# A two-block float32 transformer on one core: VectorE and ScalarE work in another order around the output projections and the recurrent preparation, with fewer unread products

## The chip, the cores and the metric

One core of a Trainium2 chip runs the whole program in one launch. The time is device microseconds (us) of that launch. In the profile PE is TensorE's matmuls, PEld its weight loads, DVE is VectorE, ACT ScalarE, POOL GpSimd, SP SyncE.

## The reference

Two residual blocks run over a sequence of 256 positions of width 1024. The change touches the end of the first block's mixer and the first layer of the second:

```python
merged = jax.nn.sigmoid(gate_a) * (y_a @ w_a_out) + jax.nn.sigmoid(gate_b) * (y_b @ w_b_out)
return merged @ w_out
...
y = h @ w_in                                   # second block, 272 positions
ys = ys + (prev - ys) * mu
r, k, v, wd, ad, gd = jnp.split(ys, RWKV_SPLITS, axis=-1)
decay = jnp.exp(-jnp.exp(wlog))
kk = kk / jnp.maximum(jnp.linalg.norm(kk, axis=-1, keepdims=True), 1e-12)
kf = kf * (1.0 + (a - 1.0) * k_a)
...
S = S * w_t + sa[..., None] * (kk_t * a_t) + v_t[..., None] * k_t
o = jnp.einsum('bhvk,bhk->bhv', S, r_t)
...
bonus = jnp.sum(rf * kf * r_k, axis=-1, keepdims=True) * vf
o = (o + bonus) * g
```

Everything is float32. The reference steps through the positions one by one; the kernel takes them in chunks of 128, 128 and 16 with a triangular inverse per head.

## The kernel before, in words

**Weights.** All weights come as slabs of 8 x 128 rows by 256 columns through a ring of four buffers `raw`. ScalarE rounds a slab to the high part (`split_hi`, L465), VectorE subtracts to get the low part (`split_lo`, L473), and TensorE makes three products per tile: high by high, low activation by high weight, high activation by low weight (`pe_pairs`, L560 to L562), 48 for a slab. There are two buffers of `w_hi` and `w_lo`, so a slab can be split as soon as the one two before it has been multiplied (`slab_done`). A section of a projection is a list of slabs; the slab with number u fills two PSUM banks, which must have been emptied (`act_took`, `dve_took`) two slabs before.

**Order.** The order is written out by hand: each engine has its own program, and semaphores tie them together. `act_pairs` and `dve_pairs` write one section for ScalarE and VectorE: for each slab u they split the next slab and then take the outputs of slab u-1. ScalarE and VectorE run what they are given strictly in this order.

**Output projections** (about 510 to 612 us). Sections `a_out` (four half slabs), `b_out` (four slabs) and `w_out` (four). VectorE multiplies the outputs of `a_out` with their gate (`gated_a`, L2079) and so frees their banks; it makes the low half of `y_b` in two halves (`low_b`, L2098) from `yb_hi`, which ScalarE writes (L2024). TensorE begins `b_out` with tiles in order, three products each, and waits at a tile for its low half `yb_l`. For each slab of `b_out`, `gated_b` multiplies the outputs by their gate into `tmp_b` (L2115), adds (`merged`, L2118), waits for ScalarE's rounded copy `x_hi` (`high`, L2032), and subtracts to `x_lo` (L2120). `w_out` begins tile by tile behind these.

**Recurrent preparation** (to 892.9 us). Sections `ev_s` (seven slabs) and `ev_u` (two). ScalarE copies outputs out (`copy`, L2268), VectorE mixes each position with the one before it (`shifted`, L2324 and L2326); beside them stand a norm of `kk` (a reciprocal square root on ScalarE, L2301, then three VectorE operations, L2367 to L2370), the decays (four exponentials on ScalarE, L2294 to L2298), and at the end six products on VectorE and the bonus product on `v_t` (L2382). After `ev_u` TensorE makes 28 products that nobody reads (`HATS_BUSY`, L527, `keep_busy`).

**Recurrent block** (893.2 to 999 us). VectorE makes `hats`, ScalarE copies two Gram matrices into `rb_at` (L2698), VectorE begins the inverse (`begin`, L1021 to L1028), then five levels follow: products `products_p`, masks on VectorE, a further Gram matrix (`later`), products `products_y`, `grow`. Unread products stand in the waits: `TURN_BUSY` 3 at each level and 12 more at the first, which with 3 make the 15 of one row. Then come three steps (`step_of`), each: right side, `ww` solve, new state, outputs `oo`; with `STEP_BUSY` = 8 unread products behind the right side, 8 behind the solve, 8 before the outputs, and one within each second head of the outputs.

## Time and profile before

| | us |
|---|---|
| median of 3 runs | 1616.67 (1611.66 to 1644.3) |
| the profiled execution, its own time | 1619.03 |
| its span, first to last instruction | 1617.2 |
| mean granted TensorE clock | 0.988 of full |

Busy time of an engine is time with an instruction in it. An idle interval in brackets names what ended it. `PEq` or "issue" means that no data dependency is shown for it. Matmul ends are modelled; their starts, and the starts of the weight loads, are what a pace is read from.

### The profile page before, as it was taken

To read this page: it belongs to the slowest core of one execution; us is meant where nothing else is said; L and a number is where in the kernel's file an instruction comes from. 1 tells how busy PE (TensorE), PEld (TensorE's weight loads), DVE (VectorE), ACT (ScalarE), POOL (GpSimd) and SP (SyncE) were. 2 spreads that over 40 slices of the span, in tenths; PEclk is the share of its full clock that TensorE was granted. 3 is DMA by queue.
4 is the path that set the end of the run, shared out by engine and by line. 5 is a ranking of instruction groups with operands and counts; after the bars stand their busy time and mean duration, and the time that the engine had idled before them with its cause. 6 is when DMAs were issued, how large, how long until landed. Compare 5 with 4: busy or idle time off the path is not lost. (4 is left out here: it accounts for less than half of the span.)

```text
span 1617.2 us, 33845 instructions
## 1 busy us (share of the span) xinstructions
PE 1541.4 (95%) x14269; PEld 1486.2 (92%) x14269; DVE 1042.7 (64%) x1584; ACT 741.4 (46%) x1024; POOL 61.1 (4%) x82
## 2 busy tenths in 40 slices
PE   5999999999999899999999999999999998899997
PEld 5999998999999898999989998999998987799997
DVE  7999546998754768444488855645446666565544
ACT  2555435695214734444356022566333354456532
POOL 0111000000110000110000100000000000000000
PEclk9999999999999999999999999999999999999999
DMA  9899645543213446555443002354452431245551
GB/s 376 302 357 355 233 170 186 183 157 119 74 61 105 169 157 234 183 182 189 177 132 117 10 2 76 109 182 161 177 183 87 145 117 52 79 157 182 184 187 47
DMA packets 39201, 256.88 MB, mean 159 GB/s; under 512 B 4259, under 2 KB 5668, under 8 KB 9892
## 3 DMA queue, kind: packets, MB, share of 16 engines
q1 hardware_dynamic: 37492, 251.07, 43.1%
q10 hardware_dynamic: 1584, 3.97, 0.6%
q8 instruction: 100, 1.64, 0.4%
q14 instruction: 25, 0.20, 0.0%
HBM read 251.87 MB, written 3.15 MB: 158 GB/s over the span
## 5 line engine op out<-in xcount | busy, mean ns | idle before, releaser
L473 DVE TENSOR_TENSOR w_lo<-raw,w_hi 128x2048 fp32r<-128x2048 f32 (+2 forms) x203 | 456.3, 2248 | 407.6 <-ACT w_hi L465 407.1
L560 PE MATMUL bank<-x_hi,w_hi 128*128 128x256 f32 (+1 forms) x1832 | 524.9, 287 | 17.6 <-DVE w_lo L473 7.4
L465 ACT ACTIVATE w_hi<-raw 128x2048 fp32r<-128x2048 f32 (+2 forms) x203 | 381.7, 1880 | 315.0 <-PE bank L562 291.1
L562 PE MATMUL bank<-x_hi,w_lo 128*128 128x256 f32 (+1 forms) x1832 | 516.8, 282 | 0.0
L561 PE MATMUL bank<-x_lo,w_hi 128*128 128x256 f32 (+1 forms) x1832 | 516.3, 282 | 0.0
L560 PEld LDWEIGHTS bank<-x_hi,w_hi 128*128 128x128 f32 x1832 | 345.9, 189 | 26.2 <-issue 16.3
L562 PEld LDWEIGHTS bank<-x_hi,w_lo 128*128 128x128 f32 x1832 | 348.1, 190 | 0.0
L561 PEld LDWEIGHTS bank<-x_lo,w_hi 128*128 128x128 f32 x1832 | 346.3, 189 | 0.9 <-issue 0.7
L560 PE MATMUL bank<-mh_hi,w_hi 128*128 128x272 f32 (+1 forms) x512 | 145.6, 284 | 0.0
L562 PE MATMUL bank<-mh_hi,w_lo 128*128 128x272 f32 (+1 forms) x512 | 145.6, 284 | 0.0
L561 PE MATMUL bank<-mh_lo,w_hi 128*128 128x272 f32 (+1 forms) x512 | 145.5, 284 | 0.0
L560 PE MATMUL bank<-hid_hi,w_hi 128*128 128x256 f32 x352 | 98.8, 281 | 1.6 <-DVE w_lo L473 1.6
L561 PE MATMUL bank<-hid_lo,w_hi 128*128 128x256 f32 x352 | 98.3, 279 | 0.0
L562 PE MATMUL bank<-hid_hi,w_lo 128*128 128x256 f32 x352 | 98.3, 279 | 0.0
L562 PEld LDWEIGHTS bank<-mh_hi,w_lo 128*128 128x128 f32 x512 | 97.3, 190 | 0.0
L560 PEld LDWEIGHTS bank<-mh_hi,w_hi 128*128 128x128 f32 x512 | 96.2, 188 | 0.0
L561 PEld LDWEIGHTS bank<-mh_lo,w_hi 128*128 128x128 f32 x512 | 96.2, 188 | 0.0
L560 PEld LDWEIGHTS bank<-hid_hi,w_hi 128*128 128x128 f32 x352 | 66.6, 189 | 2.4 <-issue 2.4
L1173 ACT ACTIVATE hid_hi<-hid 128x256 f32 (+1 forms) x44 | 18.4, 418 | 105.5 <-DVE hid L1214 105.5
L561 PEld LDWEIGHTS bank<-hid_lo,w_hi 128*128 128x128 f32 x352 | 66.3, 188 | 0.0
L562 PEld LDWEIGHTS bank<-hid_hi,w_lo 128*128 128x128 f32 x352 | 66.3, 188 | 0.0
L3178 PE MATMUL bank<-x_hi,w_hi 128*128 128x272 f32 (+1 forms) x192 | 61.4, 320 | 4.9 <-DVE k_at L3316 3.4
(593 smaller groups left out, 2525.0 us busy)
## 6 DMA issues: line engine op xcount, KB each, us to landing
raw<-in_stream SPq DMA_DIRECT2D x227, 1024.0 KB, 4.8
raw<-in_stream SPq DMA_DIRECT2D x8, 768.0 KB, 4.0
gate_store<-stage ACTq DMA_DIRECT2D x8, 256.0 KB, 2.5
raw<-in_stream SPq DMA_DIRECT2D x4, 512.0 KB, 3.4
h<-in_h ACTq DMA_DIRECT2D x1, 1088.0 KB, 9.1
zt<-gate_store SPq DMA_DIRECT2D x1, 1024.0 KB, 5.5
gate<-gate_store SPq DMA_DIRECT2D x1, 1024.0 KB, 7.7
out<-h SPq DMA_DIRECT2D x8, 128.0 KB, 1.9
```

Source lines behind the costliest of these rows:

```text
L465: nc.scalar.activation(w_hi[:, s_at % 2, 0:kt], raw[:, r_at % RING, 0:kt], ACT.Copy).then_inc(hi_done, 1)
L473: nc.vector.tensor_tensor(w_lo[:, s_at % 2, 0:kt], raw[:, r_at % RING, 0:kt], w_hi[:, s_at % 2, 0:kt].bitcast(F32), ALU.subtract).then_inc ...
L560: nc.tensor.matmul(out, hi, xh[:, k0 + k, 0:L], start=start, stop=False)
L561: nc.tensor.matmul(out, hi, xl[:, k0 + k, 0:L], start=False, stop=False)
L562: mm = nc.tensor.matmul(out, lo, xh[:, k0 + k, 0:L], start=False, stop=stop)
L1173: nc.scalar.activation(hid_hi[:, bass.ds(n, 1)], hid[:, b:b + 1], ACT.Copy).then_inc(hid_h, 1)
L3178: nc.tensor.matmul(out, hi, x_hi[:, k, cols], start=k == 0, stop=False)
```

## The change

In the output projections: `b_out` begins in three phases (all high by high products, then all low by high, then all by the low weights), each with its own wait; `gated_a(2)` goes ahead of both `low_b`, and both go ahead of the low weights of `b_out`; in `b_out` the gates of a slab go ahead of the split of the next one, and the next slab's high part on ScalarE goes ahead of the last `high`. In the preparation: the root of `kk` goes ahead of the exponentials on ScalarE; its three VectorE operations go ahead of the last `shifted` and of the split; the bonus product goes to the recurrent block, behind `hats`. There the first later Gram matrix uses banks 2 and 3, the inverse begins half by half, the last split of `ev_u` moves from the beginning to level 3 and the window part 3 (`v_t`) behind the levels. Unread products: `HATS_BUSY` 28 to 4, the 12 at level 0 gone, behind the right side 8 to 3 (`SOLVE_BUSY`), before and within the outputs 10 to 0 in each of two steps: 24 + 12 + 10 + 20 = 66 fewer. Nothing that is computed changes.

```diff
-TURN_BUSY, FIRST_TURN_BUSY, HATS_BUSY, STEP_BUSY, END_BUSY, OUT_BUSY, MIX_BUSY = 3, 12, 28, 8, 24, 14, 26
+TURN_BUSY, FIRST_TURN_BUSY, HATS_BUSY, SOLVE_BUSY, STEP_BUSY, END_BUSY, OUT_BUSY, MIX_BUSY = 3, 12, 4, 3, 8, 24, 14, 26
...
-        def pe_pairs(pe, sec, xh, xl, L, after=None, norm=None, tile_ready=None, U=2, busy=0, begun=(), by_tiles=False, busy_bank=7, lead=None):
...
                     r, r_at, s, s_at, _ = numbers(sec, i, U, u, g)
+                    if phases and i is None and u == 0:
+                        pe.wait_ge(hi_done, s + 1)
+                        for phase, (part, x) in enumerate(((w_hi, xh), (w_hi, xl), (w_lo, xh))):
+                            if phase == 2:
+                                pe.wait_ge(raw_used, r + 1 + RING)
+                            for k in range(kt):
+                                if phase < 2:
+                                    phases[phase](k)
+                                for j in range(2):
+                                    mm = nc.tensor.matmul(out_bank(sec, u, j)[:, 0:L], part[:, s_at % 2, k, j * P:(j + 1) * P], x[:, k, 0:L],
+                                                          start=phase == 0 and k == 0, stop=phase == 2 and k == kt - 1)
+                        mm.then_inc(slab_done, 1)
+                        continue
...
+            def begin_chunk(self, dve, c):
...
+                for r in self.quads:
+                    mask = masks[r, 0, self.target, 0:half][:, None, :, None].broadcast_to([self.W, self.nh, half, 1])
+                    ins = nc.vector.tensor_tensor(joined(self.y[r, c, :, 0:self.W], 0, self.target), joined(self.a_t[r, c, 0:self.nh, r], 0, self.target), mask, ALU.mult)
+                ins.then_inc(self.on.y_half, 1)
+                nc.vector.tensor_copy(joined(y, 0, self.source), joined(eye, 0, self.source))
+                dve.wait_ge(self.on.y_half, a0["half"] + c + 1)
+                nc.vector.tensor_tensor(joined(y, 0, self.target), joined(eye, 0, self.target), joined(y, 0, self.target), ALU.subtract).then_inc(self.on.y_mid, 1)
+                dve.wait_ge(self.on.y_mid, a0["mid"] + c + 1)
+                nc.vector.transpose(self.x[rows, c, :, 0:self.W], y).then_inc(self.on.y_done, 1)
...
-                act_pairs(act, S["b_out"], high, ahead=True)
+                act_pairs(act, S["b_out"], high, ahead=True, whole=False)
+                split_hi_ahead(act, S["w_out"])
+                high(None, 3, 0)

                 def square_h(i, u, U):
                     taken(act, S["w_out"], None, u, 0)
                     norm_ffn2.square(act, u, sq_f)
-                act_pairs(act, S["w_out"], square_h)
+                act_pairs(act, S["w_out"], square_h, ahead=True)
...
-                pe_pairs(pe, S["b_out"], yb_hi, yb_lo, T1, tile_ready=lambda k: pe.wait_ge(yb_l, k // 4 + 1), by_tiles=True)
+                pe_pairs(pe, S["b_out"], yb_hi, yb_lo, T1, tile_ready=lambda k: None,
+                         phases=(lambda k: pe.wait_ge(yb_h, k // 4 + 1), lambda k: pe.wait_ge(yb_l, k // 4 + 1)))
...
+                gated_a(2)
                 low_b(0)
+                low_b(1)
                 split_lo(dve, (S["b_out"], 0, numbers(S["b_out"], None, 0, 0, 0)))
-                low_b(1)
-                gated_a(2)
                 gated_a(3)
                 split_lo_ahead(dve, S["b_out"])
...
                     for j in range(2):
...
                     ins.then_inc(dve_took, 1)
                     taken(dve, S["b_out"], None, u, 0)
                     nc.vector.tensor_tensor(merged[:, 2 * u:2 * u + 2], merged[:, 2 * u:2 * u + 2], tmp_b[:, u % 2], ALU.add).then_inc(m_done, 1)
+
+                def low_merged(u):
                     dve.wait_ge(m_h, u + 1)
                     nc.vector.tensor_tensor(x1_lo[:, 2 * u:2 * u + 2], merged[:, 2 * u:2 * u + 2], x1_hi[:, 2 * u:2 * u + 2].bitcast(F32), ALU.subtract).then_inc(m_l, 1)
-                dve_pairs(dve, S["b_out"], gated_b, ahead=True)
+                for u in range(4):
+                    gated_b(u)
+                    if u < 3:
+                        split_lo(dve, following(S["b_out"], None, 4, u + 1, 0, u == 2))
+                    low_merged(u)
+                split_lo_ahead(dve, S["w_out"])
...
-                dve_pairs(dve, S["w_out"], residual)
+                dve_pairs(dve, S["w_out"], residual, ahead=True)
...
+                        act.wait_ge(q["kk_ms"], 1)
+                        nc.scalar.activation(e2[:], e1[:], ACT.Abs_reciprocal_sqrt).then_inc(q["kk_y"], 1)
                         act.wait_ge(q["ex"], 1)
                         nc.scalar.activation(g_fin[:], g_fin[:], ACT.Exp, scale=-DECAY)
                         nc.scalar.activation(reset[:], log_g[:], ACT.Exp, scale=DECAY).then_inc(q["ex_done"], 1)
                         act.wait_ge(q["ex_done"], 1)
                         nc.scalar.activation(log_g[:], log_g[:], ACT.Exp, scale=-DECAY).then_inc(q["ex_done"], 1)
                         nc.scalar.activation(log_w[:], log_w[:], ACT.Exp, scale=-DECAY).then_inc(q["ex_done"], 1)
-                    if n == 6:
-                        act.wait_ge(q["kk_ms"], 1)
-                        nc.scalar.activation(e2[:], e1[:], ACT.Abs_reciprocal_sqrt).then_inc(q["kk_y"], 1)
...
-                dve_pairs(dve, S["ev_s"], shifted, beside)
+                dve_pairs(dve, S["ev_s"], shifted, beside, whole=False)
                 dve.wait_ge(q["kk_y"], 1)
                 link(dve, "dve", nc.vector.tensor_tensor(e3[:], e2[:], e2[:], ALU.mult))
-                split_lo(dve, following(S["ev_u"], None, 2, 0, 0, False))
                 link(dve, "dve", nc.vector.scalar_tensor_tensor(out=e3[:], in0=e3[:], scalar=-0.5, in1=e1[:], op0=ALU.mult, op1=ALU.mult))
                 link(dve, "dve", nc.vector.scalar_tensor_tensor(out=e3[:], in0=e3[:], scalar=1.5, in1=e2[:], op0=ALU.add, op1=ALU.mult))
+                shifted(None, 6, 0)
+                split_lo(dve, following(S["ev_u"], None, 2, 0, 0, False))
...
-                dve.wait_ge(q["vr_mm"], 3)
-                for k in range(RW):
-                    dve.wait_ge(q["bon_mm"], k + 1)
-                    nc.vector.tensor_tensor(v_t[:, k], v_t[:, k], banks[4 + k][:, 0:T2], ALU.mult)
...
         LATER = [(1, 0), (2, 0), (3, 0), (1, 1), (2, 1), (3, 1)]
+        LATER_BANKS = [(2, 3)] + [(6, 7)] * 5
...
-                        idle_slab(1, STEP_BUSY)
+                        idle_slab(1, SOLVE_BUSY)
...
-                    if makes_state:
-                        idle_slab(5, STEP_BUSY)
...
-                        if k % 2:
-                            idle_slab(0, 1)
...
-                for c in range(2):
-                    pe.wait_ge(m["hat"], c + 1)
-                    gram(0, c, ((2, 3), (6, 7))[c])
+                pe.wait_ge(m["hat"], 1)
+                gram(0, 0, (2, 3))
+                pe.wait_ge(m["hat"], 2)
+                pe.wait_ge(m["bonus"], 1)
+                gram(0, 1, (6, 7))
                 for l in range(LEVELS):
                     if l == 0:
                         pe.wait_ge(m["gr2_out"], 2)
-                        pe.wait_ge(m["gr_act"], 4)
-                    if l:
+                        pe.wait_ge(m["gr_act"], 2)
+                        pe.wait_ge(m["hat"], 4)
+                    else:
                         idle_slab(0, TURN_BUSY)
                         big.products_p(pe, l)
-                    if l == 0:
-                        pe.wait_ge(m["hat"], 4)
-                    else:
+                        pe.wait_ge(m["gr_act"], 4)
                         pe.wait_ge(m["gr_out"], 2 * l)
-                    gram(*LATER[l], (6, 7))
-                    if l == 0:
-                        idle_slab(0, 4 * TURN_BUSY)
+                    gram(*LATER[l], LATER_BANKS[l])
...
+                for k in range(RW):
+                    ins = nc.vector.tensor_tensor(v_t[:, k], v_t[:, k], banks[4 + k][:, 0:T2], ALU.mult)
+                ins.then_inc(m["bonus"], 1)
...
-                split_lo(dve, following(S["ev_u"], None, 2, 1, 0, True))
-                dve.wait_ge(m["gr_act"], 4)
-                big.begin(dve)
+                for c in range(2):
+                    dve.wait_ge(m["gr_act"], c + 3)
+                    big.begin_chunk(dve, c)
...
-                    if l < 4:
+                    if l < 3:
                         windows(l)
+                    if l == 3:
+                        split_lo(dve, following(S["ev_u"], None, 2, 1, 0, True))
                     if l == 4:
                         rescaled(0)
                 big.crossed(dve)
+                windows(3)
```

VectorE at the opening of `b_out`, before (`gate` x4 is `gated_a(2)` and `gated_a(3)`, `yb_lo` the two `low_b`, `w_lo` a slab's low part, `tmp_b`, `gate`, `x_lo` slab 0 of `gated_b`):

```order
L473 TENSOR_TENSOR w_lo<-raw,w_hi 128x1024
L2079 TENSOR_TENSOR gate<-gate,bank 128x256 x2
L2072 TENSOR_TENSOR o_sum<-o_sum,zt 128x1024
L2098 TENSOR_TENSOR yb_lo<-o_sum,yb_hi 128x1024
L473 TENSOR_TENSOR w_lo<-raw,w_hi 128x2048
L2098 TENSOR_TENSOR yb_lo<-o_sum,yb_hi 128x1024
L2079 TENSOR_TENSOR gate<-gate,bank 128x256 x4
L473 TENSOR_TENSOR w_lo<-raw,w_hi 128x2048 x2
L2115 TENSOR_TENSOR tmp_b<-gate,bank 128x256 x2
L2118 TENSOR_TENSOR gate<-gate,tmp_b 128x512
```

and after:

```order
L473 TENSOR_TENSOR w_lo<-raw,w_hi 128x1024
L2110 TENSOR_TENSOR gate<-gate,bank 128x256 x2
L2103 TENSOR_TENSOR o_sum<-o_sum,zt 128x1024
L2110 TENSOR_TENSOR gate<-gate,bank 128x256 x2
L2129 TENSOR_TENSOR yb_lo<-o_sum,yb_hi 128x1024 x2
L473 TENSOR_TENSOR w_lo<-raw,w_hi 128x2048
L2110 TENSOR_TENSOR gate<-gate,bank 128x256 x2
L473 TENSOR_TENSOR w_lo<-raw,w_hi 128x2048
L2146 TENSOR_TENSOR tmp_b<-gate,bank 128x256 x2
L2149 TENSOR_TENSOR gate<-gate,tmp_b 128x512
```

`gated_a(2)` and both `low_b` now stand ahead of the low weights of `b_out`'s first slab; the second slab's follow `gated_a(3)`, the third's follow the first slab's gates and stand ahead of its `x_lo`.

VectorE at the end of the preparation, before (`shift` and `Y` are `shifted`, `e` the three operations of the norm, `w_lo` the first slab of `ev_u`):

```order
L2362 SCALAR_TENSOR_TENSOR bonus<-Y,vec 128x272 x4
L473 TENSOR_TENSOR w_lo<-raw,w_hi 128x2048
L2324 TENSOR_TENSOR shift<-Y 128x544
L2326 SCALAR_TENSOR_TENSOR Y<-shift,vec,Y 128x272 x2
L2324 TENSOR_TENSOR shift<-Y 128x544
L2326 SCALAR_TENSOR_TENSOR Y<-shift,vec,Y 128x272 x2
L2367 TENSOR_TENSOR e<-e 128x1088
L473 TENSOR_TENSOR w_lo<-raw,w_hi 128x2048
L2369 SCALAR_TENSOR_TENSOR e<-e 128x1088
L2370 SCALAR_TENSOR_TENSOR e<-e 128x1088
```

and after:

```order
L2399 SCALAR_TENSOR_TENSOR bonus<-Y,vec 128x272 x4
L473 TENSOR_TENSOR w_lo<-raw,w_hi 128x2048
L2361 TENSOR_TENSOR shift<-Y 128x544
L2363 SCALAR_TENSOR_TENSOR Y<-shift,vec,Y 128x272 x2
L2404 TENSOR_TENSOR e<-e 128x1088
L2405 SCALAR_TENSOR_TENSOR e<-e 128x1088
L2406 SCALAR_TENSOR_TENSOR e<-e 128x1088
L2361 TENSOR_TENSOR shift<-Y 128x544
L2363 SCALAR_TENSOR_TENSOR Y<-shift,vec,Y 128x272 x2
L473 TENSOR_TENSOR w_lo<-raw,w_hi 128x2048
```

The three `e` now come ahead of the last `shifted`, and the split behind it, ahead of `kk_t`.

TensorE ahead of the outputs of the first step, before (L924 is the small inverse, L527 the unread products, L2591 and L2592 the outputs):

```order
L2568 MATMUL bank<-acc,rows_kb 128x128
L2569 MATMUL bank<-v_rw,rows_kb 128x128
L924 MATMUL bank<-rinv_y,rprod 16x8 x8
L924 MATMUL bank<-rinv_x,rb_at 16x8 x8
L527 MATMUL bank<-w_hi 128x256 x8
L2591 MATMUL bank<-acc,rb_t 128x64
L2592 MATMUL bank<-v_rw,rk_t 128x64
L2591 MATMUL bank<-acc,rb_t 128x64
L2592 MATMUL bank<-v_rw,rk_t 128x64
```

and after:

```order
L2603 MATMUL bank<-acc,rows_kb 128x128
L2604 MATMUL bank<-v_rw,rows_kb 128x128
L937 MATMUL bank<-rinv_y,rprod 16x8 x8
L937 MATMUL bank<-rinv_x,rb_at 16x8 x8
L2622 MATMUL bank<-acc,rb_t 128x64
L2623 MATMUL bank<-v_rw,rk_t 128x64
```

The eight products ahead of the outputs and the one behind each second head are gone.

## Rows read from the trace of the kernel before

**Rows 1.** Page, part 1: busy time, share of the span, instructions
```profile
PE 1541.4 (95%) x14269; PEld 1486.2 (92%) x14269; DVE 1042.7 (64%) x1584; ACT 741.4 (46%) x1024; POOL 61.1 (4%) x82
```

**Rows 2.** Timeline of the weight loads, 549 to 565, then 570 to 590
```profile
552.03 0.19 PEld L562 LDWEIGHTS bank<-ya_hi,w_lo 128*128 128x128 f32 x1
555.59 0.29 PEld L560 LDWEIGHTS bank<-yb_hi,w_hi 128*128 128x128 f32 x1 [3.37 <-DVE gate L2079]
...
574.06 0.19 PEld L560 LDWEIGHTS bank<-yb_hi,w_hi 128*128 128x128 f32 x1 [0.56 <-DVE tmp_b L2115]
...
580.24 0.19 PEld L560 LDWEIGHTS bank<-x_hi,w_hi 128*128 128x128 f32 x1 [0.46 <-DVE tmp_b L2115]
...
585.13 0.19 PEld L560 LDWEIGHTS bank<-x_hi,w_hi 128*128 128x128 f32 x1 [0.72 <-DVE x_lo L2120]
...
588.59 0.19 PEld L560 LDWEIGHTS bank<-x_hi,w_hi 128*128 128x128 f32 x1 [2.00 <-issue]
```

**Rows 3.** Stretches: length, busy times, granted clock, DMA share and GB per second
```profile
556.00:560.00 4.00, 4.00 (x25) 4.00 (x25) 2.40 (x2) 3.15 (x3) 0.00 (x0) 0.65 0.73 248
560.00:564.00 4.00, 4.00 (x37) 4.00 (x37) 0.00 (x0) 1.09 (x1) 0.00 (x0) 1.00 0.58 233
590.00:600.00 10.00, 10.00 (x78) 10.00 (x78) 3.91 (x4) 2.55 (x2) 0.00 (x0) 0.85 0.52 203
966.00:975.00 9.00, 8.95 (x123) 8.55 (x123) 4.51 (x18) 0.63 (x1) 0.00 (x0) 1.00 0.01 2
992.00:999.00 7.00, 6.33 (x30) 5.79 (x28) 5.61 (x16) 1.67 (x4) 0.00 (x0) 0.52 0.00 0
```

**Rows 4.** Timeline of VectorE, then ScalarE, at the opening of b_out
```profile
551.46 2.28 DVE L473 TENSOR_TENSOR w_lo<-raw,w_hi 128x2048 fp32r<-128x2048 f32 x1
553.66 1.22 DVE L2098 TENSOR_TENSOR yb_lo<-o_sum,yb_hi 128x1024 fp32r<-128x1024 f32 x1
554.80 1.41 DVE L2079 TENSOR_TENSOR gate<-gate,bank 128x256 f32<-128x256 f32 x4
...
551.09 1.04 ACT L2024 ACTIVATE yb_hi<-o_sum 128x1024 fp32r<-128x1024 f32 x1
```

**Rows 5.** Timeline of VectorE, then ScalarE, as w_out begins
```profile
584.38 0.69 DVE L2120 TENSOR_TENSOR x_lo<-gate,x_hi 128x512 fp32r<-128x512 f32 x1 [0.70 <-ACT x_hi L2032]
586.18 2.29 DVE L473 TENSOR_TENSOR w_lo<-raw,w_hi 128x2048 fp32r<-128x2048 f32 x1 [1.11 <-ACT w_hi L465]
...
584.26 1.90 ACT L465 ACTIVATE w_hi<-raw 128x2048 fp32r<-128x2048 f32 x1
```

**Rows 6.** Timeline of VectorE, ScalarE and TensorE at the preparation's end
```profile
879.05 2.29 DVE L473 TENSOR_TENSOR w_lo<-raw,w_hi 128x2048 fp32r<-128x2048 f32 x1 [0.58 <-ACT w_hi L465]
...
891.38 1.47 DVE L2382 TENSOR_TENSOR Y<-Y,bank 128x272 f32<-128x272 f32 x4
...
874.74 1.28 ACT L2301 ACT_TABLE_LOAD   x1
...
889.25 3.66 PE L527 MATMUL bank<-x_hi 128*128 128x256 f32 x28
```

**Rows 7.** Timeline of VectorE and TensorE as the recurrent block begins
```profile
900.33 0.85 DVE L1021 TENSOR_TENSOR rinv_y<-rb_at,cst 64x256 f32<-64x256 f32 x2 [2.04 <-ACT rb_at L2698]
...
902.90 2.06 PE L527 MATMUL bank<-w_hi 128*128 128x256 f32 x15
```

**Rows 8.** Timeline of TensorE and VectorE in the first step
```profile
951.05 1.21 PE L527 MATMUL bank<-w_hi 128*128 128x256 f32 x8
...
957.97 1.21 PE L527 MATMUL bank<-w_hi 128*128 128x256 f32 x8
...
959.82 0.37 PE L527 MATMUL bank<-w_hi 128*128 128x256 f32 x1
960.03 0.33 PE L2591 MATMUL bank<-acc,rb_t 128*128 128x64 f32 x2
...
950.67 0.69 DVE L2795 COPY acc<-bank 128x512 f32<-128x512 f32 x1 [4.89 <-PE bank L2544]
```

More of the change, by code:

```diff
@@ L527, in keep_busy, with pe_pairs @@
                 nc.tensor.matmul(banks[bank][:, 0:moving.shape[-1]], stationary, moving, start=True, stop=True)
-        def pe_pairs(pe, sec, xh, xl, L, after=None, norm=None, tile_ready=None, U=2, busy=0, begun=(), by_tiles=False, busy_bank=7, lead=None):
+        def pe_pairs(pe, sec, xh, xl, L, after=None, norm=None, tile_ready=None, U=2, busy=0, begun=(), by_tiles=False, busy_bank=7, lead=None, phases=None):
             if norm:
@@ L1028, in begin @@
                     nc.vector.transpose(self.x[rows, c, :, 0:self.W], self.y[rows, c, :, 0:self.W]).then_inc(self.on.y_done, 1)
+            def begin_chunk(self, dve, c):
+                a0, rows, half = self.at0, slice(0, self.C), self.W // 2
+                eye = const("eyes")[rows, 0:self.W][:, None, :].broadcast_to([self.C, self.nh, self.W])
+                masks = const("levels").rearrange("p (l f n) -> p l f n", l=LEVELS, f=2)
+                y = self.y[rows, c, :, 0:self.W]
+                for r in self.quads:
[7 more added lines that the diff above has]
+                nc.vector.transpose(self.x[rows, c, :, 0:self.W], y).then_inc(self.on.y_done, 1)
             def masked(self, dve, l):
@@ L2102, in _, with gated_b @@
                 times_z(1)
+                gated_a(2)
                 low_b(0)
+                low_b(1)
                 split_lo(dve, (S["b_out"], 0, numbers(S["b_out"], None, 0, 0, 0)))
-                low_b(1)
-                gated_a(2)
                 gated_a(3)
                 split_lo_ahead(dve, S["b_out"])
-                def gated_b(i, u, U):
-                    outputs_ready(dve, S["b_out"], i, u, U)
+                def gated_b(u):
+                    outputs_ready(dve, S["b_out"], None, u, 0)
                     dve.wait_ge(gate_act, 2)
@@ L2449, in build @@
         z_pool = over_lo[:, 0:4 * T2].rearrange("p (k n) -> p k n", k=4)
-        names = ("hat", "gr", "gr2", "gr2_out", "gr_act", "gr_out", "hat2", "kb_mm", "kb_out", "rr", "rr_out", "ww", "ww_out", "oo", "oo_out", "st", "st_out", "bd0",
+        names = ("hat", "bonus", "gr", "gr2", "gr2_out", "gr_act", "gr_out", "hat2", "kb_mm", "kb_out", "rr", "rr_out", "ww", "ww_out", "oo", "oo_out", "st", "st_out", "bd0",
                  "pw", "d2", "d2_sq", "ms", "y", "nrm", "tr", "o_done", "pl", "pl_mm", "z_done", "z_hi", "z_lo", "o_hi", "v_b", "g_w",
@@ L2729, in later @@
                         dve.wait_ge(m["gr"], 4 + 2 * l + par + 1)
-                        nc.vector.tensor_tensor(dst[:, par, RW * c:RW * c + RW], heads4(banks[6 + par]),
+                        nc.vector.tensor_tensor(dst[:, par, RW * c:RW * c + RW], heads4(banks[pair[par]]),
                                                 const(mask)[:, None, :].broadcast_to([P, RW, P]), ALU.mult).then_inc(m["gr_out"], 1)
```

1 line of the change is left out of this document (added).

## The prediction

> **What bounds the kernel now.** I read the page's busy times first: TensorE has an instruction in 95% of the span, VectorE in 64%, ScalarE in 46% [rows 1]. Some 76 us without a product are all that an order can win on TensorE; to these come the stretches at the half clock, and products that nobody reads where they stand on the path. So the second view is the timeline of the weight loads, cut down to the rows with idle time ahead of them, in each place that the change touches; the third is the table of stretches with the granted clock; the last are the timelines of VectorE and ScalarE beside each of these waits, to see what stood ahead of the instruction that ended it.
>
> In the output projections the reader is to see five waits [rows 2]: 3.37 us as `b_out` opens, 0.56 and 0.46 for `tmp_b`, 0.72 for `x_lo`, 2.00 on "issue" as slab 1 of `w_out` begins. Behind the first and the last the clock is down: 556 to 560 holds 25 products at a granted 0.65 where the next 4 us hold 37 at 1.00, and 590 to 600 holds 78 at 0.85 [rows 3]. At 1.00 a product takes 4.00 / 37 = 0.108 us, so these falls cost (37 - 25) x 0.108 = 1.3 us and (92.5 - 78) x 0.108 = 1.6 us.
>
> **The output projections, opening.** `b_out` waits for the gate of `a_out`'s outputs, which frees its banks. VectorE does that from 554.80 to about 555.5, and ahead of it stand the split at 551.46 (2.28 us) and `low_b(1)` at 553.66 (1.22) [rows 4]. In the new order `gated_a(2)` is ahead of all three. Counting with these durations from when VectorE takes up the first `low_b` (551.46 - 1.22 = 550.2): half of the four gates 0.7 (to 550.9), `low_b(0)` to 552.1, `low_b(1)` to 553.35 (its `yb_hi` is done at 551.09 + 1.04 = 552.13), split 2.28 to 555.6, `gated_a(3)` to 556.3, split of slab 1 to 558.6. TensorE starts as `a_out` ends, 552.2: 16 products high by high at 0.108 end by 554.0, 16 with the low half (there since 553.35) by 555.7, 16 with the low weights, ready at 555.6, by 557.5. So the wait of 3.37 and the fall of 1.3 go, and slab 1 is late next: its low weights come at about 558.6. The order of VectorE work alone makes that wait; counted from the same rows with a little slack for products that pace slower, I take 0.9. Bounds: 0.4 if `gated_a(3)` overlaps nothing but the splits run shorter, 1.5 if the clock does not hold through 552 to 558. Gain 3.4 + 1.3 - 0.9 = 3.8.
>
> **The same, b_out and w_out.** The gates of a slab no longer stand behind the next split, so both `tmp_b` waits go: 0.56 + 0.46 = 1.0 [rows 2]. The split they now stand ahead of is needed a slab (5.2 us) later and takes 2.3, which covers it. As `w_out` opens, ScalarE writes `x_hi` for slab 3 first (it ends at 584.3) and then the weights' high half at 584.26 for 1.90; VectorE takes the low half at 586.18, after waiting 1.11 for ScalarE, and ends at 588.47, where TensorE resumes at 588.59 [rows 2, 5]. Moved ahead of that `high`, the weights' high half starts when its buffer is free, as slab 3 of `b_out` gets under way, and the low half follows without ScalarE's 1.11; what remains late is about 0.3, the `low` of slab 3 now being ahead of it. The moved `high` costs `x_lo` of the last tiles up to ScalarE's 1.90; they are the last tiles that slab 0 of `w_out` reads, 6 tiles x 6 products x 0.108 = 3.9 us after its start, and that covers it. Without the cover it would cost 1.9. Gain 0.7 + 2.0 - 0.3 + the fall of 1.6 = 4.0. Bounds: 2.4 if the clock falls all the same, 4.3 if nothing is left of the 0.3.
>
> **The preparation.** Its end is VectorE's: the bonus products, four of together 1.47 us, run from 891.38 to 892.85, and 28 unread products of TensorE, 3.66 us from 889.25, end at 892.91 beside them [rows 6]. Both must be shorter for the next block to start sooner. Now VectorE ends 1.47 sooner by the bonus products, which move behind `hats` in the next block, where VectorE waited 2.04 us for `rb_at` [rows 7]; and it no longer stands still for the norm's root, whose ScalarE operation goes ahead of four exponentials. I take 2.3 for that, an estimate between nothing and the 3.66 of the stretch that covered it (the table load of 1.28 and an exponential or two that the root no longer waits behind), 3.8 in all: to 889.1. TensorE: 4 of 28 products are left, 4 x 0.131 = 0.5, so 889.25 + 0.5; but its slab of `ev_u` has to wait for a split that `shifted` now stands ahead of. At 879.05 it began after 0.58 of waiting [rows 6] and takes 2.29; a start 0.4 later passes to TensorE's end, 890.2 with a little for the queue. The later of the two is TensorE: 892.9 - 890.3 = 2.6. The root and the exponentials share ScalarE with a table load of 1.28 [rows 6]; the reorder puts the root between functions of another table, one load more. It lies ahead of exponentials that VectorE reads only behind `kk_t`: hidden; if not, 1.3 less. Bounds: 1.2 to 3.8.
>
> **The opening of the recurrent block.** 12 unread products go out of the 15 that take 2.06 us at 902.90 [rows 7], 12 x 0.137 = 1.6. The inverse's start is VectorE's, though: the split of 2.3 us leaves it, the bonus 1.5 comes in, the start runs half by half. VectorE and not these products sets when level 1 begins, so I take 0.7, with 0 and 1.6 + 0.8 (split less bonus) = 2.4 as ends. The split, at 2.3, now stands at level 3 where `windows(3)` stood, beside products; and `windows(3)`, behind the levels, comes before the first step where VectorE waited 4.89 us for TensorE at 950.67 [rows 8].
>
> **The steps.** Behind the right side stand 8 products at 951.05, 1.21 us; VectorE's copy that ends the real wait runs 950.67 to 951.36 [rows 8]. Three products, 0.4 us, end at 951.45: all 5 removed were behind the wait, 5 x 0.131 = 0.65 us (0.131 is 3.66 / 28). Ahead of the outputs stand 8 at 957.97 with nothing to wait for, 8 x 0.131 = 1.05, and one within each second head: from 959.82 to the output behind it at 960.03, 0.2, twice a step [rows 8]. Per step 0.65 + 1.05 + 0.4 = 2.1, in two steps 4.2. Bounds: 2.6 if the next step's VectorE work is what is waited for (then only the right side's and half of the rest count), 4.6 with the modelled 1.21 instead.
>
> **A rule against this.** In the rows the dense stretch of the step, 966 to 975, has 123 products at a granted 1.00, and the last one, 992 to 999, made of few and small products, 30 at 0.52 [rows 3]: what a stretch is filled with does bear on the clock here. The Trainium skill, page Perfetto Trace Analysis, section Matmul Optimizations, says the engine "dynamically scales power based on utilization, so it's important that matmuls execute back-to-back in batches"; by that rule, taking fillers out may cost more than they did, and the rows agree in so far as both levels stand beside these fillings. By the rows alone the steps stay dense behind the removed places (outputs and new state follow at once), so I keep 4.2; by the rule the sum would be the first rival's.
>
> **Sum.** 3.8 + 1.0 + 4.0 + 2.6 + 0.7 + 4.2 = 16.3. The profiled execution took 1619.03 (span 1617.2, 1.8 outside it): 1602.7 on its scale. It was 2.4 above the median of the runs, so on theirs 1600.3; I say 1600.
>
> **Rivals.** (1) *Slower: the steps run at the half clock.* Place: the two steps with a state, 950 to 992, whose waits now hold fewer products. A product at the level of 0.52 takes twice 0.108, so each us of products that was at full pace costs one more. Of the 42 us I count 25 as products that would pay (an estimate: the rest are small products, paced by their issue): +25 - 16.3 gives +9, or 1626; it decides from 16 us of products at half on. For it: the 0.52 at the end [rows 3]. Against: 966 to 975 holds small products of the outputs and of the new state already, and is at 1.00 [rows 3]. (2) *The waits are passed on and the clock falls anyway.* The two falls (2.9) remain beside a shorter wait, and preparation and opening give 1.5 of 3.3: 16.3 - 2.9 - 1.8 = 11.6, or 1605. For it: the new wait of 0.9 stands 5 us behind an old one. Against: 37 products at 1.00 directly behind the fall [rows 3]. (3) *A fall elsewhere goes too.* The last stretch, 992 to 999, is at 0.52 beside VectorE's chain; earlier or denser arrival could keep it up: half of its 5.8 us of products is 2.9, or 1597. For: nothing but that the steps end tighter. (4) *The change does nothing that can be measured*: the gaps were idle beside another bound; with TensorE at 95% [rows 1] little speaks for it: 1616.
>
> **How the numbers follow.** Forecast 0.60, rival 1 0.06, rival 2 0.20, rival 3 0.11, rival 4 0.03. The sum's own bounds, taken together by half (each term's ends seldom fall on one side), are 1595 to 1606; with rival 2's tail and rival 3's, 1592 to 1609, which leaves out rivals 1 and 4 and the outermost of the bounds, under 2 in 10. A measurement tells about 2% from no change, 32 us: faster by that needs twice the sum, 0.02; slower by it needs more than rival 1 with its whole price, 0.02; within it 0.96.
>
> **What would show it.** In the profile after: no idle ahead of `b_out`'s first load, about 0.9 ahead of its second slab and a granted clock near 1 for 552 to 560; no `tmp_b` waits; under 0.5 ahead of slab 1 of `w_out`; the recurrent block begins 11 to 12 us earlier than 893 (8.8 + 2.6); each step 2 us shorter. Wrong if the clock in the steps is under 0.9, if a wait of over 2 us stands at slab 1 of `b_out`, or if the block's start moved by under 8 us.

## The result and the profile after

The changed kernel took 1630.29 us (median of 4 runs, 1625.89 to 1634.42) against 1614.16 of the kernel before (median of 4, 1610.45 to 1644.30): ratio 1.0109 with a 95% interval of 1.0078 to 1.0139, so 1.1% slower, where 1% faster was forecast. The profiled execution took 1634.42 us, its span is 1632.6.

Page, parts 1 and 2, of the kernel after: busy times, then the granted clock in 40 slices:

```profile
PE 1559.4 (96%) x14203; PEld 1503.4 (92%) x14203; DVE 1045.3 (64%) x1584; ACT 743.4 (46%) x1025; POOL 61.5 (4%) x82
...
PEclk9999999999999999999999569999999999999999
```

The first line answers to [rows 1]: 66 products fewer (14203 for 14269), and TensorE busy 18.0 us longer. That pair says at once that products have become slower, not that something waits. The clock row says where: slices 23 and 24 of 40, from 898 to 980 us, are at 5 and 6 tenths, where the kernel before has a 9 in every slice.

In the output projections every wait went as forecast. Timeline of the weight loads, 549 to 581, of the kernel after:

```profile
551.97 1.89 PEld L552 LDWEIGHTS bank<-yb_hi,w_hi 128*128 128x128 f32 x16
553.78 1.89 PEld L552 LDWEIGHTS bank<-yb_lo,w_hi 128*128 128x128 f32 x16
555.59 1.89 PEld L552 LDWEIGHTS bank<-yb_hi,w_lo 128*128 128x128 f32 x16
558.47 0.19 PEld L573 LDWEIGHTS bank<-yb_hi,w_hi 128*128 128x128 f32 x1 [0.99 <-issue]
...
580.64 0.19 PEld L573 LDWEIGHTS bank<-x_hi,w_hi 128*128 128x128 f32 x1 [0.33 <-issue]
```

Timeline of VectorE beside it, kernel after:

```profile
550.23 0.74 DVE L2110 TENSOR_TENSOR gate<-gate,bank 128x256 f32<-128x256 f32 x2
550.89 2.40 DVE L2129 TENSOR_TENSOR yb_lo<-o_sum,yb_hi 128x1024 fp32r<-128x1024 f32 x2
553.21 2.28 DVE L473 TENSOR_TENSOR w_lo<-raw,w_hi 128x2048 fp32r<-128x2048 f32 x1
555.41 0.74 DVE L2110 TENSOR_TENSOR gate<-gate,bank 128x256 f32<-128x256 f32 x2
556.07 2.28 DVE L473 TENSOR_TENSOR w_lo<-raw,w_hi 128x2048 fp32r<-128x2048 f32 x1
```

`b_out` begins as `a_out` ends, its three phases follow one another without a gap, and of the waits of [rows 2] two are left: 0.99 us for the low weights of slab 1, which end at 558.35 and were put at 558.6, and 0.33 as slab 1 of `w_out` begins.

In the recurrent block it is the clock. Stretches of the kernel after (columns as in [rows 3]):

```profile
556.00:560.00 4.00, 3.18 (x28) 3.01 (x28) 3.71 (x5) 3.97 (x4) 0.00 (x0) 1.00 0.82 283
...
888.00:892.00 4.00, 3.61 (x64) 3.10 (x62) 3.84 (x10) 0.24 (x1) 0.95 (x1) 1.00 0.02 4
892.00:896.00 4.00, 3.33 (x41) 3.27 (x43) 3.97 (x7) 0.00 (x0) 0.00 (x0) 0.53 0.00 0
...
904.00:920.00 16.00, 16.00 (x221) 15.36 (x221) 7.62 (x22) 0.00 (x0) 1.05 (x2) 0.50 0.01 2
...
968.00:972.00 4.00, 4.00 (x49) 3.90 (x47) 1.11 (x5) 1.71 (x3) 0.00 (x0) 1.00 0.00 0
```

and the stretch of the same length and clock time in the kernel before:

```profile
904.00:920.00 16.00, 16.00 (x381) 15.07 (x381) 13.85 (x31) 0.00 (x0) 2.00 (x4) 1.00 0.01 2
```

TensorE is busy for all 16 us in both. At a granted 1.00 it starts 381 products in them, at 0.50 it starts 221. The clock falls from 1.00 to 0.50 (from 2.4 to 1.2 GHz) at about 892 and comes back at about 967, when the whole inverse is over. The engine's work ahead of the fall and behind it, and at the return, in the timeline of TensorE of the kernel after:

```profile
887.34 1.71 PE L2518 MATMUL bank<-kk_t,Y 64*128 64x128 f32 x16
888.98 0.96 PE L2522 MATMUL bank<-kk_t,hats 64*64 64x64 f32 x16
889.87 0.62 PE L527 MATMUL bank<-w_hi 128*128 128x256 f32 x3
890.52 1.12 PE L937 MATMUL bank<-rinv_x,rb_at 64*64 64x32 f32 x32
892.67 1.92 PE L937 MATMUL bank<-rinv_x,rb_at 64*64 64x32 f32 x32 [1.02 <-DVE rinv_x L1056]
894.51 3.09 PE L2518 MATMUL bank<-Y,nb_t 64*128 64x128 f32 x16
...
964.65 3.42 PE L2537 MATMUL bank<-over_x,pool_w 128*128 128x272 f32 x8
967.92 1.89 PE L2579 MATMUL bank<-v_rw,ak_t 128*128 128x64 f32 x16
```

16 products of a Gram matrix take 1.71 us ahead of the fall and 3.09 behind it. The clock returns inside the eight products of 272 columns (0.50 from 966.5 to 967, 0.63 in the next half microsecond, then 1.00). And there is a wait that is new: 1.02 us between the halves of the level 1 products, for VectorE's second half of the begin, where 15 unread products stood before [rows 7].

Three distances make the balance, before and after: to the start of the recurrent block 893.21 and 881.15, 12.1 us shorter; from there to the right side of the first step (the row at 948.74 in the kernel before, 967.92 now) 55.5 and 86.8, 31.2 longer; from there to the first output tile of the next section (981.22 and 997.25) 32.5 and 29.3, 3.2 shorter. -12.1 + 31.2 - 3.2 = 15.9, where the spans differ by 15.4.

The ratios leave out the longest executions where a kernel has two kinds, here the one of 1644.30 us of the kernel before, whose clock is not on record, and below 3 of 10 of `b_no12` (1642 to 1649 us) and 4 of 10 of `b_hats4` (1647 to 1655), whose mean clock of 0.959 to 0.966 is as low as the 0.964 to 0.967 of the changed kernel.

### The profile page after: what moved, and what is told of

Same layout as the page of the kernel before. It is cut to its first block and busy times, and to the rows that moved or that the text cites. A ratio compares the mean times of both kernels' runs of the same rounds, so it can differ in the third digit from the quotient of the medians.

```text
span 1632.6 us, 33719 instructions
## 1 busy us (share of the span) xinstructions
PE 1559.4 (96%) x14203; PEld 1503.4 (92%) x14203; DVE 1045.3 (64%) x1584; ACT 743.4 (46%) x1025; POOL 61.5 (4%) x82
```

## The experiments

All stand beside runs of the kernel before on the same chip; ratios are to that, with a 95% interval.

**Full products back at level 0.** Edit to the changed kernel:

```diff
                     gram(*LATER[l], LATER_BANKS[l])
+                    if l == 0:
+                        idle_slab(0, 4 * TURN_BUSY)
```

> The changed kernel with the 12 unread products at level 0 back, behind the first later Gram matrix. Theory (the stretch of small products from 881 to 892 no longer holds the full clock because the unread products are out of it): granted clock 1.00 through the levels, recurrent block about 55 us up to the first step in place of 86.8, time 1630.3 - 31 + 1 = about 1600. Rival (the half-wise begin or another moved operation brings the clock down): clock 0.50 from 892 to 965 as in the changed kernel, time about 1631. The 12 products also fill the new wait of 1.02 us, so this run alone does not tell a filled wait from more work.

Measured: 1599.23 us, ratio 0.9923 (0.9899 to 0.9947). Stretch and timeline of TensorE of this kernel:

```profile
888.00:892.00 4.00, 3.96 (x85) 3.68 (x84) 3.93 (x8) 0.00 (x0) 0.00 (x0) 1.00 0.00 0
...
948.00:952.00 4.00, 4.00 (x33) 3.86 (x33) 1.44 (x6) 0.00 (x0) 0.00 (x0) 0.50 0.01 4
```

```profile
877.39 0.39 PE L2639 MATMUL bank<-kk_t,nb_t 64*16 64x16 f32 x13 [0.30 <-PEq L2294]
...
886.11 2.05 PE L527 MATMUL bank<-w_hi 128*128 128x256 f32 x15
...
932.61 1.89 PE L2579 MATMUL bank<-v_rw,ak_t 128*128 128x64 f32 x16
```

Twelve products of some 1.6 us are worth 31: the block's start to its first step is 932.61 - 877.39 = 55.2 us again, and all nine executions lie between 1597 and 1608. The row at 0.50 shows a second, shorter fall, in the steps; it comes up again below.

**As many products, but ahead of the block.** Edit to the changed kernel:

```diff
-... HATS_BUSY, SOLVE_BUSY, ... = 3, 12, 4, 3, 8, 24, 14, 26
+... HATS_BUSY, SOLVE_BUSY, ... = 3, 12, 28, 3, 8, 24, 14, 26
```

> The changed kernel with 28 unread products in place of 4 behind the preparation; level 0 still has no 12. Theory: if it is the amount of full products ahead that counts, the clock stays at 1.00 and the time is 1630.3 - 31 + 3 = about 1602. Rival (the idle time of 1.02 us ahead of the second half of the first products is what brings it down): the wait is still there, the clock is 0.50 from there on and the time about 1633.

Measured: 1636.86 us, ratio 1.0147 (1.0108 to 1.0185). Timeline and stretches of this kernel:

```profile
873.61 3.66 PE L527 MATMUL bank<-x_hi 128*128 128x256 f32 x28
...
889.09 1.12 PE L937 MATMUL bank<-rinv_x,rb_at 64*64 64x32 f32 x32 [1.02 <-DVE rinv_x L1056]
```

```profile
888.00:892.00 4.00, 2.83 (x52) 2.69 (x48) 3.93 (x8) 0.00 (x0) 0.00 (x0) 0.95 0.00 0
892.00:896.00 4.00, 4.00 (x70) 3.78 (x71) 3.39 (x7) 0.00 (x0) 0.00 (x0) 0.50 0.02 4
```

28 full products that end at 877 do not hold the clock up to 892: it falls at 891.6, with TensorE at work. So my first theory, in its form "how many ahead", fell; it left the two things that stand right before the fall, the idle time and the small products, which the next pair tells apart.

**The new wait filled, with full and with small products.** Both edits go into the changed kernel, between the two halves of the level 1 products:

```diff
-                        big.products_p(pe, l)
+                        big.products_p(pe, l, (lambda: idle_slab(5, 8)) if l == 1 else None)
```

```diff
+                def small_idle():
+                    s = S["ev_out"].s0 % 2
+                    for n in range(32):
+                        nc.tensor.matmul(banks[5][0:64, 0:32], w_hi[0:64, s, 0, 0:64], w_hi[0:64, s, 1, 0:32], start=True, stop=True)
...
-                        big.products_p(pe, l)
+                        big.products_p(pe, l, small_idle if l == 1 else None)
```

> The changed kernel with 8 unread full products (128 x 128 by 256) between the two halves of the level 1 products, where the new wait of 1.02 us stands, and nothing else. Theory (what is in the last few us before 892 decides, the idle wait among it): the clock stays at 1.00, 8 x 0.131 = 1.05 fit the wait, time about 1598. Rival (the amount of full products over the block's opening decides, and 8 are too few where 28 ahead of the block were): clock 0.50, time about 1631.

> As the last, but 32 small unread products (64 x 64 by 32 columns, about 0.033 us each) in the same place, so that the wait is filled and no full product is added. If idle time alone brings the clock down: 1.00 through the levels, time about 1598. If what counts is how much of the array the products use: 0.50 from 892 on, about 1631.

Measured: with 8 full products 1599.16 us, ratio 0.9935 (0.9912 to 0.9957); with 32 small ones 1637.62, ratio 1.0153 (1.0119 to 1.0187). Timeline of TensorE with the full ones, its columns as above:

```profile
886.53 1.12 PE L937 MATMUL bank<-rinv_x,rb_at 64*64 64x32 f32 x32
887.59 1.21 PE L527 MATMUL bank<-w_hi 128*128 128x256 f32 x8
888.73 1.12 PE L937 MATMUL bank<-rinv_x,rb_at 64*64 64x32 f32 x32
```

Timeline and stretches with the small ones:

```profile
892.13 1.12 PE L937 MATMUL bank<-rinv_x,rb_at 64*64 64x32 f32 x32
893.19 2.96 PE L2638 MATMUL bank<-w_hi 64*64 64x32 f32 x32
896.08 1.92 PE L937 MATMUL bank<-rinv_x,rb_at 64*64 64x32 f32 x32
```

```profile
893.00:894.00 1.00, 1.00 (x24) 0.96 (x21) 0.97 (x3) 0.00 (x0) 0.00 (x0) 0.99 0.07 16
894.00:895.00 1.00, 1.00 (x12) 1.00 (x12) 1.00 (x3) 0.00 (x0) 0.00 (x0) 0.50 0.00 0
```

This is the pair that decides. The wait is gone in both: no idle time stands in brackets. With the small products TensorE is busy for the whole of both stretches, and the clock falls to 0.50 under it, from 24 products in 1 us to 12. With 8 full ones in the same place, 1.14 us from start to start, it stays through the levels. One execution of each was profiled, but all five with the full ones have a mean clock of 0.985 to 0.988 and all four with the small ones 0.960 to 0.964. So filling the idle time is not enough; of the two fillings the full products hold the clock and the small ones do not.

The two differ in the part of the array (128 x 128 for 64 x 64) and in the columns (256 for 32), and no run takes these apart. That the part of the array is not all of it shows in the steps of the kernel with the 8 full ones, where the clock falls a second time. Timeline of TensorE and stretches there:

```profile
943.32 0.62 PE L2624 MATMUL bank<-acc,rb_t 128*128 128x64 f32 x2
```

```profile
942.00:943.00 1.00, 1.00 (x12) 1.00 (x11) 0.53 (x1) 0.00 (x0) 0.00 (x0) 1.00 0.00 0
943.00:944.00 1.00, 1.00 (x9) 1.00 (x8) 0.00 (x0) 0.00 (x0) 0.00 (x0) 0.67 0.00 0
```

The row is one of sixteen of its kind that follow one another. These products use the whole array, with 64 columns each, TensorE is busy throughout, and the clock falls all the same.

**Only the begin in one piece.** Edit to the changed kernel:

```diff
-                for c in range(2):
-                    dve.wait_ge(m["gr_act"], c + 3)
-                    big.begin_chunk(dve, c)
+                dve.wait_ge(m["gr_act"], 4)
+                big.begin(dve)
```

> The changed kernel with the inverse begun for both halves at once, as before, and no unread products back. The wait of 1.02 us between the two halves goes and stands ahead of the first instead. If that wait's place decides: clock 1.00, about 1600. If the missing full products decide (theory): 0.50 from about 892, about 1632.

Measured: 1631.66 us, ratio 1.0134 (1.0088 to 1.0180). Timeline of TensorE, and a stretch, of this kernel:

```profile
886.39 2.81 PE L937 MATMUL bank<-rinv_x,rb_at 64*64 64x32 f32 x64 [1.40 <-DVE rinv_x L1041]
```

```profile
888.00:892.00 4.00, 4.00 (x40) 3.86 (x36) 3.19 (x7) 0.00 (x0) 0.00 (x0) 0.50 0.00 0
```

The wait is in another place, and 1.40 long; the clock falls all the same, at 887.4, a microsecond behind the wait.

**Orders alone, and products alone.** The change is taken in two: the changed kernel with all 66 unread products back (`orders_only`), and the kernel before with the 66 out (`fillers_only`). The edit shown is that of the second, to the kernel before; the first puts the same lines back into the changed kernel.

```diff
-TURN_BUSY, FIRST_TURN_BUSY, HATS_BUSY, STEP_BUSY, END_BUSY, OUT_BUSY, MIX_BUSY = 3, 12, 28, 8, 24, 14, 26
+TURN_BUSY, FIRST_TURN_BUSY, HATS_BUSY, STEP_BUSY, END_BUSY, OUT_BUSY, MIX_BUSY = 3, 12, 4, 8, 24, 14, 26
...
-                        idle_slab(1, STEP_BUSY)
+                        idle_slab(1, 3)
...
-                    if makes_state:
-                        idle_slab(5, STEP_BUSY)
...
-                        if k % 2:
-                            idle_slab(0, 1)
...
-                    if l == 0:
-                        idle_slab(0, 4 * TURN_BUSY)
```

> The changed kernel with all 66 unread products back. If the order is sound by itself: clock 1.00 through the block, output projections 9.5 us shorter, preparation about the same (its 28 products end after VectorE again), so 1611 - 9 = about 1602. If the half-wise begin or another moved operation brings the clock down: 1630 or more.

> The kernel before with all 66 unread products of the change removed, in the old order of all other work. If fewer unread products are enough for the loss: the clock falls at the start of the block and stays down, 1611 + 31 - 4 = about 1638. If the new order is needed as well: 1608 to 1615.

Measured: orders alone 1604.17 us, ratio 0.9970 (0.9946 to 0.9994), products alone 1647.04, ratio 1.0220 (1.0166 to 1.0274). By the ratios the orders win about 5 us (1 to 9) and the thinned products lose about 35 (27 to 44); the sum of some 30 is more than the 18 that the ratio of the whole change makes, since alone the thinned products lose more. The timeline of TensorE of the second shows why:

```profile
887.77 0.39 PE L2604 MATMUL bank<-kk_t,nb_t 64*16 64x16 f32 x13 [3.06 <-PEq L2256]
```

In the old order VectorE ends the preparation 3 us after TensorE's 4 products, and the clock is down as the first Gram matrix begins, not at level 1: 0.58 from 888 to 892.

**One set of products at a time, kernel before.**

```diff
-                    if l == 0:
-                        idle_slab(0, 4 * TURN_BUSY)
```

```diff
-TURN_BUSY, FIRST_TURN_BUSY, HATS_BUSY, STEP_BUSY, END_BUSY, OUT_BUSY, MIX_BUSY = 3, 12, 28, 8, 24, 14, 26
+TURN_BUSY, FIRST_TURN_BUSY, HATS_BUSY, STEP_BUSY, END_BUSY, OUT_BUSY, MIX_BUSY = 3, 12, 4, 8, 24, 14, 26
```

> The kernel before with the 12 unread products at level 0 removed and nothing else. Theory of both sets needed: the clock falls near 905, the time is 1614 + 28 = about 1642. Theory of either set being enough: clock stays, time 1614 - 1 = 1613.

> The kernel before with 4 in place of 28 unread products behind the preparation and nothing else. VectorE ends the preparation 0.06 us before they do, so nothing is gained by it: 1614 if the clock stays (either set is enough), about 1642 if it falls (both are needed).

Measured: without the 12 a median of 1614.75 us over all ten executions and 1613.06 over the seven in the ratio, 0.9999 (0.9966 to 1.0032); with 4 for 28 1619.85 over all ten and 1616.34 over six, ratio 1.0027 (1.0001 to 1.0053). Beside them stand the executions told of at the end of the section on the result, some 30 us longer; among the 24 of the kernel before on that chip there was none (1606 to 1620), in the first comparison one of four (1644.30). Their sizes and clocks fit a fall like that of the changed kernel, but none of them was profiled, so this is not shown.

Without the 12 the profiled execution is at 1.00 from 868 to 984: in it the 12 are not needed. `hats28` has the same unread products up to the end of the levels, in the new order, and its four executions are all at 1635 to 1640 us. So the new order has a part in the fall too; which of its moves is not tested. With 4 for 28 the clock is down in the profiled execution as well, from 890 on, but it comes back; what varies from one execution to the next may there be the return. Timeline of TensorE, then stretches:

```profile
889.21 0.39 PE L2608 MATMUL bank<-kk_t,nb_t 64*16 64x16 f32 x13 [3.06 <-PEq L2256]
...
904.81 2.93 PE L527 MATMUL bank<-w_hi 128*128 128x256 f32 x15
907.66 2.06 PE L924 MATMUL bank<-rinv_x,rb_at 64*64 64x32 f32 x64
```

```profile
900.00:904.00 4.00, 3.71 (x25) 3.52 (x27) 3.69 (x10) 0.19 (x1) 0.95 (x1) 0.50 0.00 0
904.00:908.00 4.00, 4.00 (x39) 3.74 (x36) 3.91 (x7) 0.00 (x0) 0.00 (x0) 0.65 0.02 4
908.00:912.00 4.00, 4.00 (x95) 3.84 (x94) 0.94 (x3) 0.00 (x0) 0.00 (x0) 1.00 0.00 0
```

The 15 full products at level 0 stand at the turn from 0.50 to 1.00, and the small products behind them, the same as in the changed kernel, stay at 1.00.

**Bringing it back.** Edits to the changed kernel, the second with 37 in place of 12:

```diff
-                        idle_slab(0, TURN_BUSY)
+                        idle_slab(0, TURN_BUSY + (12 if l == 2 else 0))
```

> The changed kernel with 15 in place of 3 unread full products ahead of level 2, some 11 us after the clock fell. If full products in a row bring the clock back (as 15 seemed to at 904.8 us of the run with 4 products behind the preparation): 0.50 from 892 to about 904, then 1.00 to the end of the block; of the 31 us lost about 5 stay, and the 12 products cost 2, so about 1607. If the small products of the levels hold the clock down whatever stands in one place: 0.50 to 965, 1633.

> The changed kernel with 40 in place of 3 unread full products ahead of level 2. They take 40 x 0.21 = 8.5 us at the half clock. If a long row of full products brings the clock back: 0.50 up to some point inside them and 1.00 behind, which saves about 22 of the 31 us and costs up to 8: about 1615, and in every execution alike. If not: 0.50 to the steps and 1630 + 8 = 1638.

Measured: with 15 in all 1612.36 us, ratio 1.0001 (0.9964 to 1.0038), its executions spread from 1602 to 1623; with 40 1609.35, ratio 0.9990 (0.9959 to 1.0020), from 1605 to 1615. In the profiled execution of the first the 15 (3.57 us from 894.50) did nothing: the clock stays at 0.50 up to 944. Stretches of the second:

```profile
896.00:900.00 4.00, 4.00 (x19) 4.00 (x20) 2.25 (x6) 0.00 (x0) 0.57 (x2) 0.50 0.00 0
900.00:904.00 4.00, 4.00 (x58) 3.87 (x57) 0.00 (x0) 0.00 (x0) 0.00 (x0) 0.90 0.00 0
904.00:908.00 4.00, 4.00 (x96) 3.84 (x93) 1.53 (x4) 0.00 (x0) 0.00 (x0) 1.00 0.02 4
```

The row of 40 (7.24 us from 895.82) brings the clock back inside it, and it stays for all levels. By the times, 15 are enough in some executions and not in others; how many it takes is not shown, since in the changed kernel the clock came back inside only eight, of 272 columns. Against the median of the changed kernel, from another comparison, that is 21 us won (1630.3 - 1609.4), with the 37 products' own time, 7.24 x 37 / 40 = 6.7 us, in it.

**The output projections alone.** The kernel before with the edits of `pe_pairs`, of the three engines' programs in the output projections, and no other.

```diff
+                gated_a(2)
                 low_b(0)
+                low_b(1)
                 split_lo(dve, (S["b_out"], 0, numbers(S["b_out"], None, 0, 0, 0)))
-                low_b(1)
-                gated_a(2)
...
```

> The kernel before with the new order in the output projections alone. Theory: the wait of 3.37 us, both tmp_b waits, the 2.00 and the two falls of the clock go, the next section starts 9.5 us sooner (8.8 was predicted), the recurrent block is as before: 1612 - 9 = 1603. Rival (the later sections give it back, or the clock falls elsewhere): 1608 or more.

Measured: 1603.78 us, ratio 0.9953 (0.9930 to 0.9976): 7.6 us, between 3.9 and 11.3, beside the 9.5 of the traces.

**The steps alone.** The kernel before with 3 for 8 behind the right side and none before and within the outputs.

```diff
-                        idle_slab(1, STEP_BUSY)
+                        idle_slab(1, 3)
...
-                    if makes_state:
-                        idle_slab(5, STEP_BUSY)
...
-                        if k % 2:
-                            idle_slab(0, 1)
```

> The kernel before with the unread products of the steps thinned alone (3 in place of 8 behind the right side, none before and within the outputs). Theory: 3.2 us less between the first right side and the next block, clock 1.00 in the steps: 1612 - 3 = 1609. Rival (the first one of the prediction, the steps fall to the half clock): 1630 or more.

Measured: 1612.36 us, ratio 1.0000 (0.9967 to 1.0034). In its profiled execution the steps are at 1.00 and, from the right side to the next section's first tile, 28.97 us long for 32.48, 3.5 less. Yet the ten executions run from 1602 to 1621 with mean clocks from 0.992 down to 0.978, those of the kernel before beside them stay at 0.985 or more. What the products cost is won in some executions and lost again, to a clock that is down for some us, in others; that this happens in the steps was not profiled for this kernel.

**The step products, with the clock held in the inverse.** Edits to the changed kernel with its 12 back: all step products back (`steps_back`), or 8 behind the right side and 4 new ones ahead of the second step (`steps_mid`):

```diff
+                        if makes_state:
+                            idle_slab(1, 4)
                         pe.wait_ge(m["st_out"], c)
```

> The changed kernel with the 12 products at level 0 and all unread products of the steps back; only the 24 behind the preparation stay out. If the step products hold the clock: no stretch at 0.50 in the first steps, which are 3 us longer by the products and 6 shorter by the clock than in turn12: 1599 - 3 = about 1596. If they do not: the stretch stays, 1599 + 3 = 1602.

> The changed kernel with the 12 products at level 0, 8 behind the right side, and 4 new ones ahead of the second step, where TensorE waits 0.48 us for the state; none before and within the outputs. If a filled wait is enough: 1.00 through the steps and about 1594. If the products before the outputs are needed: 0.50 in the first steps, about 1600.

Measured: all back 1601.00 us, ratio 0.9944 (0.9917 to 0.9971), and no stretch below 1.00 from 868 to 972 in its profile; the other 1605.79, ratio 0.9963 (0.9934 to 0.9993), with the stretches

```profile
940.00:944.00 4.00, 3.90 (x41) 3.87 (x41) 1.99 (x8) 0.00 (x0) 0.00 (x0) 0.82 0.00 0
944.00:948.00 4.00, 4.00 (x46) 3.86 (x47) 1.31 (x6) 0.60 (x1) 0.00 (x0) 0.50 0.01 2
```

The clock is down from about 942.5, and the 4 new products start at 946.78: in this execution they came too late to hold it, so whether a filled wait ahead of the step would is not tested. No version with the step products back is faster than `turn12` (1599.2) by more than the runs scatter. `orders_only` shows a stretch at 0.50 in the steps too, with every unread product in place, so they do not hold it for certain either. What decides in the steps stays open.

## Why the prediction was wrong

Point by point, by its own steps.

- *Output projections, opening, b_out and w_out, 8.8.* Right. The section's end came at 599.12 for 608.69, and less the 0.1 by which the two stood apart as it began (a wait of 0.97 us ends at 546.08 and at 545.98), that is 9.5 us shorter. The new wait was put at 0.9 and is 0.99; the rest of 0.3 is 0.33; both falls of the clock are gone (0.65 is 1.00 in 556 to 560, 0.85 is 1.00 in 580 to 590).
- *Preparation, 2.6.* Right: the section ahead of it ended 9.6 us sooner, the recurrent block starts 12.1 sooner, so 2.5.
- *Opening of the recurrent block, 0.7.* With the clock held through the levels, by the 12 products put back (`turn12`) or by 8 in the new wait (`gap8`), the way to the first step is 55.2 for 55.5: 0.3. The size was small anyway. But this is the step that failed: "12 unread products go out of the 15 that take 2.06 us", priced at the time they take on the path. I looked at what bounded the start of the inverse, found VectorE, and did not ask what the products did for the clock. In the new order they held it, at the entrance to five levels whose own products use half of the array or less. Without them the clock was at 0.50 from 892 to 967: 31 us lost in the place of 0.7 won.
- *Steps, 4.2.* 3.2 in the changed kernel, 3.5 in `only_steps`: VectorE's state is late next by 0.48, as the lower bound had it. In the kernels with a fall in the steps it is lost again: `turn12` has 966.44 - 932.61 = 33.8 us there, more than before.
- *Rival 1, the half clock, 0.06.* The mechanism was the right one, its place and its chance were not. I gave it to the steps, where the products are full, and not to the levels, where small products stand behind the removed ones up to the first step, 904.9 to 948.7 in the kernel before. "Against: 966 to 975 at 1.00" was evidence from the steps alone. With the place right its price could have been bounded, by these 44 us at up to twice the time; 31 were lost. That its 1626 lies near the 1630 measured is luck: its 25 us were counted in the steps, which are at 1.00 in the changed kernel (from 968 to 1004).
- *"By the rows alone the steps stay dense behind the removed places, so I keep 4.2."* Here the rule of the Trainium skill (Perfetto Trace Analysis, Matmul Optimizations) that the engine scales its power with its utilization, so that matmuls should run back to back, was weighed and set aside, and the rival that it spoke for got 0.06; it was the better guide. Of it the trace agrees that what TensorE does sets the clock (1.00 with the 8 full products, 0.50 with the 32 small ones), but back to back was not enough here: `gap_small` has its products back to back, and the clock falls.

With the fall kept off by 12 or by 8 products the time is 1599, where 1600 was forecast for the whole change. That they agree is in part luck: against the kernel before on the same chip `turn12` wins 12.4 us (8.5 to 16.3) of the 16.3 of the sum, and the forecast started from 1616.67, where that chip has 1611.95. The output projections and the preparation came as summed, the steps did not. `turn12` is faster than the kernel before, and by the two comparisons than the changed one.

## What to carry to other kernels

An unread product on the path has two prices, the time it takes and the clock it holds; before one is taken out, look at what stands behind it until the next dense stretch of full products. If that is long and made of small products, its worth can be all of that stretch at half pace, here 31 us. A wait filled with full products cost nothing here (`gap8`) and was worth more than all the orders together; and where the clock had fallen anyway, a row of 40 full products ahead of a long stretch of small ones paid for itself.

## What the runs showed of the hardware

- The granted clock fell from 1.00 to 0.50 while TensorE had an instruction in it all the time: when these were 64 x 64 by 32 columns (`gap_small`, at 894), and amid others of 128 x 128 by 64 columns (`gap8`, at 943.3).
- Entered at 0.50, the levels and the end of the inverse stayed there for 75 us in the changed kernel, with 3 full products at each level. Entered at 1.00, the same products with the same 3 stayed at 1.00: from 904 to 948 in the kernel before.
- The 28 full products that ended some 14 us ahead of the fall did not help in the changed kernel, 8 full ones in the new wait just ahead of it did.
- A row of 40 full products brought it back in the profiled execution, and the ten times suggest that it did in every one; 15 did so in one profiled execution (`b_hats4`, at 906.7) and not in another (`recover`). In the changed kernel it came back at 967 inside 8 products of 272 columns.
